# Gate products moved from the merge stage into the RWKV stage, another order in a latent RWKV job, and a rewritten front, in a fused two-block fp32 kernel

## The reference, cut to what matters

```python
p = h @ P['w_in']
p_rwkv, p_mla, p_gate = jnp.split(p, [RWKV_IN, RWKV_IN + MLA_IN], axis=-1)
y_rwkv, s_fin = rwkv_branch(p_rwkv, s0, P, emit)
...
g_rwkv, g_mla = jnp.split(jax.nn.sigmoid(p_gate + P['gate_b']), N_BRANCH, axis=-1)
merged = g_rwkv * (y_rwkv @ P['w_rwkv_proj']) + g_mla * (o @ P['w_mla_proj'])
return merged @ P['w_out'], s_fin, (k, v)
```

## Time and profile before

| what | value |
|---|---|
| median of 3 runs | 3984.3 us (3970.56, 3984.3, 3986.98) |
| the profiled execution's own time | 3969.43 us |
| its span, first to last instruction | 3967.6 us |
| PE busy | 3681.3 us, 93% of the span |
| DVE, ACT, POOL busy | 33%, 13%, 4% |
| mean granted PE clock | 0.949 |
| DMA | 551.50 MB, mean 139 GB/s |

### The profile page before, as it was taken

How to read it: one execution, slowest core, us unless ns; L and a number is a source line. 1 busy time by engine, 2 the same in 40 slices (tenths; PEclk the granted TensorE clock), 3 DMA queues, 4 the chain that set the end, 5 groups by cost and what they waited for, 6 DMA issues and landing times.

```text
span 3967.6 us, 43277 instructions
## 1 busy us (share of the span) xinstructions
PE 3681.3 (93%) x18578; PEld 2923.2 (74%) x18578; DVE 1310.8 (33%) x1922; ACT 531.9 (13%) x907; POOL 163.4 (4%) x166
## 2 busy tenths in 40 slices
PE   6999999986988879998999999999899979999979
PEld 3464555545877668887888888888788858888858
DVE  1289342225668420102312222000261261070260
ACT  1100001223434200110100000000101120101120
POOL 0020000000000100000000000000050000050000
PEclk9999989987888789999999999999899989999989
DMA  7889313102321244443444444444244403344303
GB/s 309 331 358 379 131 55 113 53 32 48 82 55 29 83 152 156 148 170 127 148 149 148 151 155 148 150 157 150 96 149 140 147 22 138 117 149 148 128 32 127
DMA packets 129225, 551.50 MB, mean 139 GB/s; under 512 B 57009, under 2 KB 59185, under 8 KB 66625
## 3 DMA queue, kind: packets, MB, share of 16 engines
q1 hardware_dynamic: 113872, 447.26, 32.2%
q10 hardware_dynamic: 15200, 101.99, 6.6%
HBM read 533.48 MB, written 15.73 MB: 138 GB/s over the span
## 4 chain that ended last, share of the span: by engine, by line
PE 60%; DVE 2%; ACT 1%; issue 1%; ACTq 0%; POOLq 0%; DVEq 0%
PE ps L429 57%; PE ps L2643 1%; PE ps L2404 0%; PE ps L2651 0%; PE ps L2399 0%; PE ps L459 0%; PE ps L2335 0%; DVE arena L2700 0%; ACT arena L2778 0%; PE ps L2385 0%; DVE arena L2856 0%; PE ps L2652 0%; DVE arena L2165 0%; DVE arena L2839 0%; DVE arena L2620 0%
## 5 line engine op out<-in xcount | busy, mean ns | idle before, releaser
L429 PE MATMUL ps<-arena,ring 128*128 128x256 f32 (+3 forms) x11392 | 2626.1, 393 | 64.7 <-issue 22.6
L429 PEld LDWEIGHTS ps<-arena,ring 128*128 128x128 f32 (+1 forms) x11392 | 2172.1, 191 | 515.3 <-issue 214.0
L718 DVE SCALAR_TENSOR_TENSOR arena<-arena,small 128x512 f32<-128x512 f32 x240 | 194.2, 809 | 22.5 <-DVE arena L718 9.2
L2148 DVE TENSOR_TENSOR arena<-ps,arena 128x1024 f32<-128x1024 f32 x12 | 14.3, 1220 | 396.9 <-ACT arena L2134 396.9
L2523 DVE SCALAR_TENSOR_TENSOR arena<-arena,col 128x255 f32<-128x255 f32 (+29 forms) x180 | 108.2, 601 | 6.4
L561 PE MATMUL ps<-arena 128*128 128x512 f32 (+1 forms) x224 | 91.7, 558 | 5.3 <-ACT arena L614 5.3
L2267 DVE TENSOR_TENSOR arena<-ps,arena 128x1024 f32<-128x1024 f32 x11 | 13.5, 1224 | 239.2 <-PE ps L429 239.0
L2531 POOL TENSOR_TENSOR arena<-arena 128x1024 f32<-128x1024 f32 x2 | 4.7, 2352 | 2034.2 <-ACT arena L2472 2034.2
L1839 DVE TENSOR_TENSOR arena<-arena 64x30 f32<-64x30 f32 (+14 forms) x240 | 83.8, 349 | 8.2
L2246 ACT ACT_TABLE_LOAD x11 | 14.1, 1283 | 535.1 <-DVE arena L2280 535.1
L561 PEld LDWEIGHTS ps<-arena 128*128 128x128 f32 x224 | 42.0, 196 | 55.5 <-issue 54.2
(11 more groups left out here) (399 smaller groups left out, 3059.4 us busy)
## 6 DMA issues: line engine op xcount, KB each, us to landing
ring<-in_weights SPq DMA_DIRECT2D x404, 1024.0 KB, 4.8
arena<-in_ada_late ACTq DMA_DIRECT2D x64, 1024.0 KB, 8.5
arena<-in_front ACTq DMA_DIRECT2D x8, 1024.0 KB, 9.9
arena<-in_gates SPq DMA_DIRECT2D x32, 256.0 KB, 3.7
arena<-in_x ACTq DMA_DIRECT2D x2, 2048.0 KB, 15.0
arena<-in_ctx ACTq DMA_DIRECT2D x1, 2048.0 KB, 12.4
keep_h<-arena ACTq DMA_DIRECT2D x1, 2048.0 KB, 7.5
keep_o<-arena ACTq DMA_DIRECT2D x1, 2048.0 KB, 7.3
```

The costliest lines, as they stand in the source:

```text
L429: mm = M.matmul(o, ring[:, slot, k, c0:c0 + w], rhs, start=(kc == 0), stop=(kc == ktiles * WK - 1))
L718: ins = V.scalar_tensor_tensor(part[:, b], late[:, s, k], c, part[:, b], ALU.mult, ALU.add)
```

## The change

1. **Gate products.** `GATE_EARLY` goes from 16 to 28. Pieces in RWKV: 56 instead of 32, in 14 groups of four. Job 0 has 16 pieces: eight in a new spot "own", four spread over z5, x5, x5, fin, four at fin, fin, u, u. Jobs 1 to 3 have eight: four at "own", four at z5, x5, x5, fin. Jobs 4 to 7, which had none, have four: two ahead of `merge_64` ("m64") and two at fin. The merge stage has 6 weight tiles less (404 to 398 in all) and reads 3.5 MB of partial sums instead of 2.
2. **The "own" spot** lies on PE behind the rates and decays of job n+1 and ahead of `own_products(n+1)`. ACT evicts these pieces ahead of `turn_inverse(n)` and `key_rates(n+1)`, and `own_products(n+1)` waits for that eviction. SP loads and stores for them behind the unpacking and ahead of the next pack.
3. **`key_values` is gone.** `first_products` accumulates the masked products times the values onto the old state's part in PSUM (16 + 16 matmuls for each direction's half x, ahead of z5 and behind it). Its eviction is a copy on ACT; DVE's addition (line 1850) and ACT's two copies of line 1626 are gone.
4. **Latent jobs:** DVE masks `own_products(n+1)` ahead of the rate products, and `first_products(n, 0)` waits for the latter (`tr_in`).
5. **Front:** the loads are issued as `c`, a first piece of the constants, the columns, `x`, `ctx`, the rest, each with its own semaphore; squares of `x` on DVE, of `ctx` on ACT, added in fours on DVE, so that the sums take 4 matmuls each; the norm of one input is summed ahead of the first `fold` of the adaLN rows, the other behind it.
6. **w_in:** `LATE_AT` is (8, 18, 44) instead of (8, 22, 52), and only 4 loads precede the first eviction.
7. **Latents:** `late_columns` becomes `late_rows` (16 matmuls of 512 columns, ahead of the norms, in four partition groups of the array), two evictions, and 16 matmuls of 4 columns.
8. Semaphores of the front are cleared on POOL after the w_in stage and used again.

```diff
-GATE_EARLY = 16
+GATE_EARLY = 28
...
-            for dst, src in ((view(TMP + 4096, 4096), A['ctx']), (view(TMP, 4096), A['x']),
-                             (con[:], A['constants']), (col[:], A['columns'])):
-                a.dma_start(dst, src).then_inc(loaded.sem, loaded.up(a, 16))
...
+            a.dma_start(con[:, 0:first], A['constants'][:, 0:first]).then_inc(con_in.sem, con_in.up(a, 16))
+            a.dma_start(col[:], A['columns']).then_inc(con_in.sem, con_in.up(a, 16))
+            a.dma_start(view(TMP, 4096), A['x']).then_inc(x_in.sem, x_in.up(a, 16))
+            a.dma_start(view(TMP + 4096, 4096), A['ctx']).then_inc(ctx_in.sem, ctx_in.up(a, 16))
...
                 if g == 0:
-                    p.wait_ge(loaded.sem, 4 * 16)
-                    for q in range(2):
-                        norm_of[q][0](p)
+                    norm_sum(1)
                 fold(g)
+                if g == 0:
+                    norm_sum(0)
...
-        LATE_AT = (8, 22, 52)
+        LATE_AT = (8, 18, 44)
...
+        def late_rows(p):
+
+            p.wait_ge(late_summed.sem, late_summed.due(p, 4 * LATE))
+            for b in range(LATE // 4):
+                q = 32 * (b % 4)
+                mm = M.matmul(ps[q:q + 32, 4 + b // 4, :], C('ones')[:, 0:32], part[:, b], start=True, stop=True,
+                              tile_position=(0, q))
...
-            for n in range(LATE):
-                mm = M.matmul(ps[:, 4, n:n + 1], part[:, n // 4, n % 4 * P:(n % 4 + 1) * P], C('ones')[:, 0:1],
-                              start=True, stop=True)
...
-            late_loads(a, 0, LATE_AT[0])
+            late_loads(a, 0, LATE_SLOTS)
             evict(kv[:, 0:4, :], ps[:, 0:4, :])
-            late_loads(a, LATE_AT[0], LATE_AT[1])
+            late_loads(a, LATE_SLOTS, LATE_AT[1])
...
-        MIDST = ((0,), (1, 2), (3,), (4, 5), (6, 7))
+        STEPS, LATER = ("z5", "x5", "x5", "fin"), ("fin", "fin", "u", "u")
+        GATE_GROUPS = [(0, 4, ("own",) * 4, "own"), (0, 5, ("own",) * 4, "own"), (0, 4, STEPS, "fin"), (0, 5, LATER, "u")]
+        GATE_GROUPS += [(n, *g) for n in range(1, 4) for g in ((4, ("own",) * 4, "own"), (4, STEPS, "fin"))]
+        GATE_GROUPS += [(n, 3, ("m64", "m64", "fin", "fin"), "fin") for n in range(4, 8)]
...
                 for c in range(HF):
-                    for e in (0, 64):
-                        mm = M.matmul(ps[:, 2 * x + e // 64, c * 64:(c + 1) * 64], AR[e:e + 64, b, c, 0, t],
-                                      st[e:e + 64, hf * HF + c], start=True, stop=True)
+                    o = [ps[:, 2 * x + e, c * 64:(c + 1) * 64] for e in range(2)]
+                    for e in range(2):
+                        M.matmul(o[e], AR[64 * e:64 * e + 64, b, c, 0, t], st[64 * e:64 * e + 64, hf * HF + c],
+                                 start=True, stop=False)
+                    for e in range(2):
+                        mm = M.matmul(o[e], MR[:, x, 4 * e + c, 0], vtok(n, x, 4 * e + c), start=False, stop=True)
...
                     p.wait_ge(ev['dec_in'], n + 2)
-                key_values(n)
-                if more:
-                    p.wait_ge(ev['g_in'], 2 * n + 2)
+                    gate_pieces(n, "own")
+                    if n >= 4:
+                        p.wait_ge(ev['mr_in'], mr_count(n, 4))
+                    elif gates_by(n, "own"):
+                        p.wait_ge(gate_out.sem, gates_by(n, "own")[-1] + 1)
                     own_products(n + 1)
...
                     decays(n + 1)
+                    gate_copies(n, "own")
                 turn_inverse(n)
                 if more:
                     key_rates(n + 1)
-                key_values(n)
                 merges(n)
...
-                rate_masks(n)
                 if more:
                     own_products(n + 1)
+                rate_masks(n)
+                if more:
                     key_factors(n + 1)
-                first_values(n)
...
-            pairs(p, GATE_EARLY // 8, 2, lambda kc: hX[:, 2 * WK + kc, :], bg)
-            pairs(p, 4 - GATE_EARLY // 8, 4, lambda kc: hX[:, kc, :], bg)
+            pairs(p, 3, 2, lambda kc: hX[:, 2 * WK + kc, :], bg)
+            column_block(p, bg, 0, 2, lambda kc: hX[:, 2 * WK + kc, :])
+            column_block(p, bg, 1, 4, lambda kc: hX[:, kc, :])
```

More of the change, by code:

```diff
@@ L379, in stream_weights @@
                 load(BEFORE_RWKV + s, s)
-            loads(BEFORE_RWKV + SLOTS, n_tiles - BEFORE_RWKV - SLOTS)
+            rest = (n_tiles - BEFORE_RWKV) % SLOTS
+            loads(BEFORE_RWKV + SLOTS, n_tiles - BEFORE_RWKV - SLOTS - rest)
+            for s in range(rest):
+                sp.wait_ge(slot_left.sem, slot_left.due(sp))
+                load(n_tiles - rest + s, s)
         def per_tiles(n):
@@ L565, in piece, with norm_sum @@
                     mm.then_inc(win.full[1].sem, win.full[1].up(p))
+            def norm_sum(q):
+                p.wait_ge(con_in.sem, 32)
+                p.wait_ge(sq_sum.sem, 2 - q)
+                for c in range(4):
+                    mm = M.matmul(ps[:, 5 + q, 0:T], C('ones'), xsq[q][:, c], start=(c == 0), stop=(c == 3))
+                mm.then_inc(norm_mm.sem, 1)
             def block(g, left):
@@ L603, in front_act @@
             row(0)
-            for q in range(2):
-                norm_of[q][1](a, squares=False)
+            for q in (1, 0):
+                a.wait_ge(norm_var.sem, 2 - q)
+                S.activation(rs[:, q], rs[:, q], ACT.Sqrt).then_inc(norm_root.sem, 1)
             for j in range(4):
@@ L1997, in clear_pool @@
         def clear_pool(g):
[L1998 to L2005 removed]
+            clear(g, spent)
             end_stage(g)
```

347 lines of the change are left out of this document (213 added, 134 removed).

## The result

| | before | with the change |
|---|---|---|
| median of 20 runs, us | 3978.97 (3969.76 to 3987.85) | 3987.74 (3976.56 to 3997.75) |
| the profiled execution, us | 3969.43 | 3993.33 |
| span, us | 3967.6 | 3991.5 |

The ratio is 1.0021, with a 95% interval of 1.0013 to 1.0029: 0.2% longer, and no gain. The forecast was 3938, in a range of 3902 to 3970. The two profiled executions lie near opposite ends of their runs, so their spans differ by 23.9 where the medians differ by 8.8.

The account below looks back on a forecast made before the run. TensorE was taken as the bound: merge full, RWKV with 87 us idle. Terms -41.7 - 17.7 - 2.9 - 3.8 - 9.7 + 30 = -45.8 gave 3923.6 as profiled, 3938 against the median, range 3902 to 3970.

Parts of the forecast that it names:

- Merge, -41.7: Merge stage: six of 48 tiles go at 6.95 us each, and the larger read of partial sums costs nothing.
- Front, -17.7: Front: PE's stall shrinks and DMA is late next; first projection piece at 48 us instead of 65.66.
- The third rival: Front stays bound by DMA: first piece at 62 or later, -4 instead of -17.7, 3952 in all; chance 0.08.
- w_in and latents, -16.4: w_in: two eviction waits vanish, -2.9 and -3.8; latents: fewer, wider products let MLA start earlier, -9.7.
- RWKV, +30: RWKV stage: 41.7 us of added pieces, partly hidden in 87 us of PE idle time, cost 30 net.
- Jobs 0 and 3: RWKV: job 0 hides eight pieces in PE's idle 17.59 us, +3; job 3 has more slack behind, +1.
- Jobs 1 and 2: RWKV: turn 6 and pack 7 us later, partly absorbed by DVE waits and 7 us fewer merge pieces; +3 each.
- Jobs 4 to 6: RWKV latent jobs: four new pieces each, nothing given back, first products wait for rate masks; +5, +8, +7.
- Job 7: RWKV's last job: no successor, and slack from the missing next job's products; 0.
- The slower rival: RWKV: ACT's wait for own pieces and half-speed PE cost 12 us a job, +96, 4004 in all; chance 0.03.
- The first rival: RWKV: the added pieces all fit into PE's 87 idle us, total -75.8, 3909 against the median; chance 0.17.
- U0 on ACT: RWKV: U0 eviction moves from DVE's 0.69 us addition to ACT's 0.59 us copy, worth nothing by itself.

Follow-up runs that it names:

- the mended version: The change with separate first products in latent jobs, rate masks first, own evictions behind the key rates, two weight slots, 28 blocks early: 3907.47 us, ratio 0.9832.
- the separate kernel: The change with latent jobs as before it (separate value products, no pieces), 20 blocks early, own evictions behind the key rates: 3930.15 us, ratio 0.9883.

## Why the prediction was wrong

- **Merge, -41.7:** right, 41.1.
- **Front, -17.7:** -10.7, outside its own bounds of -12 to -20, and 54.97 to 56.07 for the first piece in all traces with the new front. The step "3 MB of it are ring tiles ahead of their use, without them it is 43.5" failed: up to the first piece 54.97 us x 371 GB/s = 20.4 MB had moved, the whole of the 20.0 that the sum began with, and PE waited 6.97 us for the ring at a DMA share of 0.96. "If all of it had to land first", 51.2, was nearer. The third rival had this mechanism, with a larger price.
- **w_in and latents, -16.4:** right, -19.6 in the trace.
- **RWKV, +30:** this term failed, 93.9 in the traces, and with it the forecast. It has these steps.
  - *Jobs 0 and 3, "+3" and "+1".* +9.2 and +7.5. In job 0 the eight pieces did hide, but PE then waited 7.91 us for the factors, where the products of line 1389 had run.
  - *Jobs 1 and 2, "+3 each".* +8.2 each. The delays were right to within 0.5 us (turn +6.3, pack +20.3). The step that failed is "PE ... gets back four pieces that the merges no longer hold (7 us)", with the first products and the merges priced at full clock. PE got less back: in job 1 it was idle 3.2 us longer, and busy 5.05 us longer on the same products, at 0.83 for 0.90. I had seen that PE would have nothing for 7 us, and had even written that it would fall to 0.53 behind it, but as a rival. Moving one line takes the wait away, 18 to 25 us over the context jobs.
  - *Jobs 4 to 6, "2 at z5, 2 at the second side, 7 for the pieces, less 3".* Nearly every part was wrong; they grew by 16.8, 20.0 and 17.0. The pieces cost nothing that a trace can tell: without them the latent jobs took 261.2 instead of 257.3. The first products, priced at 1.7 us more on each side, took 6.7 us a side where 1.0 had stood. The half clock covered not 5 us but 20.8, all of the first products and half of the merges.
  - *Job 7, "0".* +7.1. It has no successor, but the merged products and their clock are on its path as well.
- **The slower rival, 0.03.** It said that ACT's wait and the half clock cost 12 us a job, +96, "and the same happens in latent jobs by the rate masks"; RWKV lost 93.9. That the totals agree is luck: the context jobs lost 8.3 each and the latent ones 15.2. The place was right in context jobs, and so was the half clock. In latent jobs the rate masks were 17 of the 61 us; undoing the merging took 37 more with the pieces in place. The chance was too low all the same. The evidence for it, 0.53 behind a wait of 3.72 us, was in the rows that the sum rested on, and I used it for a gain.
- **The first rival, "RWKV costs nothing",** was right about the pieces alone: in the mended version 28 blocks cost RWKV 5.4 us over the 422.8 of before.
- **U0 on ACT:** the sum went by 0.59 us a copy, and the copies after took that. It was not the copy but its condition that mattered: the merging that made the addition unnecessary.

What decides when the clock falls and returns is not settled. A wait of PE came ahead of some falls, but not of the two later ones in job 1 of the change, nor of the one in job 1 with the first products ahead. In latent jobs the clock was back when dense pieces ran, and late without them, but one program returned after 13 us of work in one execution and after 27 in another. That the narrow products (64 columns and less) rather than the waits bring the lower clock is a rival that fits some of these rows; no run was made to tell. Job 0 is some 4 us longer than before even with its first products ahead; the one piece more at its end and SP's longer list there are candidates that no run took apart. The front was not tried with less data ahead of the first piece.

## What to carry to other kernels

Before work is moved, ask what it did where it stood: products that look hidden in another engine's shadow may be what bridges a gap of TensorE, and an accumulation that saves an eviction can move them onto the path. Price TensorE's work behind a wait at the lower clock, wherever the trace shows that clock behind waits of the same length, and for a whole stretch, not only for the next instruction. A late transfer (the pack) cost little once TensorE had something to do until it landed: ask what the engine on the path does in the meantime. In this kernel dense matmuls paid where they filled such a gap, and their eviction had to stand behind the work that others wait for.

## What was not expected of the hardware

- PE stayed at a granted clock of 0.50 for 20.8 us in which it was busy 20.79. The Trainium skill (TensorE: Matmul & The Clock Gate, "What's actually happening") says that activity releases the throttle. The trace agrees only in part: all this time PE was busy by its records, and the clock did not rise.
- The clock fell from full to 0.50 while PE was busy without a break: with the first products ahead, 1.00 over 970 to 983 and 0.50 over 984 to 989, and PE busy 13.00 of 13.00 and 5.00 of 5.00 us.
- The same instructions in the same order took 53.4 us in one execution and 59.7 in another (job 0 of the new front alone), by the clock: from the first products on 0.75 against 0.50 over 26.7 us.
- Removing 16 pieces of dense matmuls left PE's busy time the same (214.0 and 214.2 us), and adding 12 matmuls to each of three jobs, with results that nothing reads, gave 3963.18 us in one run, 13 under the fastest of the change's twenty.
- Merged accumulation has a price of its own at full clock: 3.8 us for a side, in alternating groups of 64-row and 128-row products, against 1.01 + 3.79/2 = 2.9 us (worked out from the separate kernel's two lines) when the same products ran apart.
